# Operand sums of the feed-forward activations: where they are made, how they are loaded, and the PSUM ring of the gate and up products

## The reference, cut to what matters

```python
h = _layer_norm(x) * (1 + sc2) + sh2
a = jax.nn.silu(jnp.einsum('bsd,df->bsf', h, w_gate[l])) * jnp.einsum('bsd,df->bsf', h, w_up[l])
ffn = jnp.einsum('bsf,fd->bsd', a, w_down[l])
x = _layer_norm(ALPHA * x + (1 + g2) * ffn) * ln2_g[l] + ln2_b[l]
```

## Time and profile before

| | |
|---|---|
| Runs shown | 3025.06, 3025.84, 3032.81 us |
| Profiled execution, its own time | 3028.47 us |
| Its span from first to last instruction | 3026.7 us |
| Mean granted TensorE clock | 0.974 |
| Busy: PE, DVE, ACT, POOL | 95%, 74%, 45%, 51% of the span |

### The profile page before, as it was taken

How to read it: one execution, slowest core, us unless ns; L and a number is a source line. 1 busy time by engine, 2 the same in 40 slices (tenths; PEclk the granted TensorE clock), 3 DMA queues, 4 the chain that set the end, 5 groups by cost and what they waited for, 6 DMA issues and landing times.

```text
span 3026.7 us, 39892 instructions
## 1 busy us (share of the span) xinstructions
PE 2862.5 (95%) x13947; PEld 2399.7 (79%) x13947; DVE 2245.8 (74%) x3042; ACT 1365.1 (45%) x2442; POOL 1541.0 (51%) x1179
## 2 busy tenths in 40 slices
PE   7999998999999988999899989999999999999885
PEld 3888886666666656888799989999999978877764
DVE  5666665988888865466776688778766677799877
ACT  3111113777777765365634343434443442323344
POOL 0223321011111125578666677677766675567786
PEclk9999999999999998999999999999999999999997
DMA  7444437121312106376432345556333265567433
GB/s 260 129 132 132 132 111 191 36 70 56 82 56 70 49 22 232 109 234 227 172 111 95 127 139 177 178 175 215 107 104 101 94 222 192 200 222 244 142 125 105
DMA packets 271059, 421.93 MB, mean 139 GB/s; under 512 B 19142, under 2 KB 157063, under 8 KB 264842
## 3 DMA queue, kind: packets, MB, share of 16 engines
q1 hardware_dynamic: 270860, 419.37, 42.6%
HBM read 289.52 MB, written 129.78 MB: 139 GB/s over the span
## 4 chain that ended last, share of the span: by engine, by line
PE 39%; DVE 9%; DVEq 4%; POOL 4%; POOLq 2%; issue 2%; DMA 1%; ACT 1%; SPq 1%; ACTq 0%
PE tail_bank L2482 9%; PE tail_bank L2483 9%; PE tail_bank L2484 9%; PE tail_bank L2508 2%; PE tail_bank L2509 2%; PE tail_bank L2510 2%; PE tail_bank L2415 1%; PE tail_bank L2414 1%; PE tail_bank L2413 1%; POOL tail_rounded L2247 1%; DVE tail_plain L2739 1%; POOL tail_rounded L2226 1%; DVEq L2731 1%; DVE tail_plain L2742 1%; DVEq L2712 1%
## 5 line engine op out<-in xcount | busy, mean ns | idle before, releaser
L2226 POOL TENSOR_TENSOR tail_rounded<-tail_plain,tail_rounded 128x512 fp32r<-128x512 f32 x462 | 660.1, 1442 | 298.6 <-ACT tail_rounded L1989 298.4
L2482 PE MATMUL tail_bank<-tail_rounded 128*128 128x384 f32 x1848 | 625.6, 339 | 32.5 <-DVE tail_plain L2659 26.1
L2483 PE MATMUL tail_bank<-tail_rounded 128*128 128x384 f32 x1848 | 623.3, 337 | 0.0
L2484 PE MATMUL tail_bank<-tail_rounded 128*128 128x384 f32 x1848 | 623.0, 337 | 0.0
L1989 ACT ACTIVATE tail_rounded<-tail_plain 128x512 fp32r<-128x512 f32 x462 | 285.9, 631 | 469.0 <-PE tail_bank L2484 270.9
L2659 DVE TENSOR_TENSOR tail_plain<-tail_plain,tail_bank 128x384 f32<-128x384 f32 x462 | 248.2, 549 | 190.6 <-PE tail_bank L2484 180.3
L2482 PEld LDWEIGHTS tail_bank<-tail_rounded 128*128 128x128 f32 x1848 | 351.3, 190 | 38.5 <-issue 37.8
L2483 PEld LDWEIGHTS tail_bank<-tail_rounded 128*128 128x128 f32 x1848 | 351.7, 190 | 0.0
L2484 PEld LDWEIGHTS tail_bank<-tail_rounded 128*128 128x128 f32 x1848 | 351.5, 190 | 0.0
L1154 DVE TENSOR_REDUCE att_peak<-att_sc 128x1 f32<-128x1024 f32 x256 | 312.8, 1222 | 42.0 <-PE att_sc L966 35.5
L2508 PE MATMUL tail_bank<-tail_rounded 128*128 128x512 f32 x693 | 282.7, 408 | 47.3 <-POOL tail_rounded L2247 30.1
(11 more groups left out here) (289 smaller groups left out, 5547.4 us busy)
## 6 DMA issues: line engine op xcount, KB each, us to landing
tail_plain<-in_w_gu SPq DMA_DIRECT2D x134, 512.0 KB, 4.9
scr_a_d<-tail_plain SPq DMA_DIRECT2D x132, 192.0 KB, 2.1
tail_plain<-scr_a_d SPq DMA_DIRECT2D x18, 1024.0 KB, 5.3
scr_out_d<-tail_plain SPq DMA_DIRECT2D x18, 1024.0 KB, 4.8
tail_plain<-scr_out_d SPq DMA_DIRECT2D x18, 1024.0 KB, 6.9
proj_ada<-in_w_ada SPq DMA_DIRECT2D x16, 1024.0 KB, 6.8
held_w_hi<-scr_qs_d SPq DMA_DIRECT2D x128, 128.0 KB, 2.9
scr_h_d<-tail_plain SPq DMA_DIRECT2D x63, 256.0 KB, 4.4
```

The costliest lines, as they stand in the source:

```text
L2226: nc.gpsimd.tensor_tensor(w_lo[:, j, :], operand(F, j), w_hi[:, j, :].bitcast(F32), ALU.subtract).then_inc(wlo_done, 1)
L2482: nc.tensor.matmul(dst, w_hi[:, j, cols], h_hi(b, j)[:, k, :], start=(k == 0), stop=False)
L2483: nc.tensor.matmul(dst, w_hi[:, j, cols], h_lo(b, j)[:, k, :], start=False, stop=False)
L2484: m = nc.tensor.matmul(dst, w_lo[:, j, cols], h_hi(b, j)[:, k, :], start=False, stop=(k == 3))
```

## The change

It does five things.

- **Sums.** `sums_a(G)` is new and runs once a step on DVE, behind `multiply(G, 3)`. Its four operations of 128x384 make s3, a21 + a22, s2 and s4 from the four blocks in `sils[G % 2]`; s3, s2 and s4 are written over three of the four blocks of `up`. `sums2` and its 27 calls are gone.
- **Stores.** `store_a` stores seven blocks a step instead of four. The first `take_u` of the next up phase waits until the three sums of the step before are stored (`s_stored`), since it writes over them. `a_d` gets the layout operand, row, pair.
- **Loads.** `load_a(r)` loads one operand of one unit (256 KB or 192 KB) into a ring of 12 places; each place is free when POOL has made the low half of the operand 12 back. 189 loads instead of 27. ACT waits for its operand's load instead of for a sum.
- **PSUM ring.** The products of gate and up go through six banks at first (24 products) and then all eight, in one sequence with those of the down stage. `place_read` gives PE the event that frees a bank, and `part_taken` counts the takes in place of the four `bank_read`.
- **rstd.** `rstd(u)` does both tiles of a unit in one set of three operations on two columns. It waits for the variance of both. `normalise(u, c)` waits for that.

```diff
-        a_in = [cut_plain(at, P, "t n", t=4, n=4) for at in (0, 4096)]
-        s2, s3, s4 = (ahead[:, i, :].rearrange("p (t z) -> p t z", z=P) for i in range(3))
+        a_in = [plain[:, at + i * 512:at + (i + 1) * 512] for at in (0, 4096) for i in range(4)] + [ahead[:, i, :] for i in range(4)]
+        SLOTS = len(a_in)
+        SUM_PLACE = ((1, 1), (0, 1), (1, 0))
...
+        def ring_place(n):
+
+            return 2 + n % 6 if n < 24 else (n - 22) % 8
...
             def store_a(G):
...
+                sp.wait_ge(asum_done, 4 * G + 1)
+                store(2, sums[0]).then_inc(s_stored, 16)
+                sp.wait_ge(asum_done, 4 * G + 2)
+                store(5, sil[:, 0, 1, :]).then_inc(a_stored[G % 2], 16)
+                sp.wait_ge(asum_done, 4 * G + 3)
+                store(1, sums[1]).then_inc(s_stored, 16)
+                sp.wait_ge(asum_done, 4 * G + 4)
+                store(6, sums[2]).then_inc(s_stored, 16)
...
-            def load_a(u):
-
+            def load_a(r):
+
+                u, p = divmod(r, OPERANDS)
                 c, q = divmod(u, QUEUE)
...
-                    sp.wait_ge(a2lo_done, OPERANDS * (u - 1))
...
+                elif r >= SLOTS:
+                    sp.wait_ge(a2lo_done, r - SLOTS + 1)
...
             for u in range(UNITS):
-                if u + 2 < UNITS:
-                    load_a(u + 2)
+                for r in range(SLOTS + OPERANDS * u, min(SLOTS + OPERANDS * (u + 1), OPERANDS * UNITS)):
+                    load_a(r)
...
-            def rstd(u, c):
-                n = tile_number(u, c)
-                at = mv[:, n % 4, :]
-                pool.wait_ge(var_done, n + 1)
-                nc.gpsimd.tensor_scalar(at[:, 2:3], at[:, 1:2], 1.0 / D, EPS, ALU.mult, ALU.add)
+            def rstd(u):
+                n = tile_number(u, 1)
+                at = mv[:, n % 4:n % 4 + 2, :]
+                pool.wait_ge(var_done, n + 2)
+                nc.gpsimd.tensor_scalar(at[:, :, 2], at[:, :, 1], 1.0 / D, EPS, ALU.mult, ALU.add)
...
-                    bank = j % 4
-                    if j == 4:
-                        pe.wait_ge(x_done, F + 1)
-                    elif j > 4:
-                        pe.wait_ge(bank_read[bank], 2 * F + 1)
-                    elif F:
-                        pe.wait_ge(bank_read[bank], F if bank in (0, 3) else 2 * F)
-                    dst = gu[:, bank, 0:HALF]
+                    if OPERANDS * F + j > 1:
+                        pe.wait_ge(*place_read(OPERANDS * F + j))
+                    dst = part_bank(F, j)
...
+            def sums_a(G):
+
+                a11, a21, a12, a22 = (sils[G % 2][:, i, c, :] for i, c in ((0, 0), (0, 1), (1, 0), (1, 1)))
+                s3, s2, s4 = (up[:, i, c, :] for i, c in SUM_PLACE)
                 dve.drain()
+                nc.vector.tensor_tensor(s3, a11, a21, ALU.subtract).then_inc(asum_done, 1)
                 dve.drain()
+                nc.vector.tensor_tensor(a21, a21, a22, ALU.add).then_inc(asum_done, 1)
                 dve.drain()
+                nc.vector.tensor_tensor(s2, a21, a11, ALU.subtract).then_inc(asum_done, 1)
+                dve.drain()
+                nc.vector.tensor_tensor(s4, a12, s2, ALU.subtract).then_inc(asum_done, 1)
...
                 if 0 < G < END:
                     sums_w(F + 2)
-                if G == END:
-                    sums2(0)
+                if G:
+                    dve.wait_ge(s_stored, 48 * G)
                 take_u(F + 1, up)
...
                 multiply(G, 3)
+                sums_a(G)
                 beside(4)
...
-                if u + 1 < UNITS:
-                    sums2(u + 1)
```

More of the change, by code:

```diff
@@ L1408, in fourier_to_end @@
         prod_done, x_done, silu_done = s.sem("prod_done"), s.sem("x_done"), s.sem("silu_done")
-        bank_read = [s.sem(f"bank{i}_read") for i in range(4)]
+        part_taken = s.sem("part_taken")
         mult_done = s.sem("mult_done")
@@ L1522, in a2_raw, with place_read, part_bank @@
         def a2_raw(p, u):
-            n, tile = pairs_in(u), a_in[u % 2]
-            return (tile[:, 0:n, 0], s2[:, 0:n], s3[:, 0:n], tile[:, 0:n, 1], tile[:, 0:n, 3], tile[:, 0:n, 2], s4[:, 0:n])[p]
+            return a_in[(OPERANDS * u + p) % SLOTS].rearrange("p (t z) -> p t z", z=P)[:, 0:pairs_in(u)]
         def a2_ready(p, u):
-            if p in (0, 3, 4):
-                return a2_landed[u % 2], 16 * (u // 2 + 1)
-            return s_done, 4 * u + {2: 1, 5: 2, 1: 3, 6: 4}[p]
+            r = OPERANDS * u + p
+            return a2_landed[r % SLOTS], 16 * (r // SLOTS + 1)
         def a2_free(p, u):
             return (down_done, OPERANDS * (u - 1) + p + 1) if u else (prod_done, OPERANDS * (PHASES - 1) + A_FREE[p])
+        def ring_place(n):
+            return 2 + n % 6 if n < 24 else (n - 22) % 8
+        def place_read(n):
+            before = [m for m in range(max(0, n - 8), n) if ring_place(m) == ring_place(n)]
+            if not before:
+                return {2: (tp_done, NT - 4), 3: (tp_done, NT - 4), 4: (gated1, NT - 1), 5: (gated1, NT - 1)}.get(
+                    ring_place(n), (h2_done, NT) if ring_place(n) < 2 else (gated1, NT))
+            if before[-1] < FIRST_DOWN:
+                F, j = divmod(before[-1], OPERANDS)
+                return (part_taken, (OPERANDS - 1) * F + j) if j else (x_done, F + 1)
+            u, p = divmod(before[-1] - FIRST_DOWN, OPERANDS)
+            return (taken, (OPERANDS - 1) * u + p) if p else (first_done, u + 1)
+        def part_bank(F, j):
+            return bank[:, ring_place(OPERANDS * F + j), 0:HALF]
         def out_bank(n):
-            return bank[:, (6, 7, 0, 1, 2, 3, 4, 5)[n % 8], :]
+            return bank[:, ring_place(FIRST_DOWN + n), :]
         def out_place(u):
@@ L1862, in step @@
                         load_piece(m)
-                    load_a(0)
-                    load_a(1)
+                    for r in range(SLOTS):
+                        load_a(r)
                     for m in range(STAGE, 4 * OPERANDS):
@@ L2024, in silu @@
             def silu(G, i, c):
-                bank, reads = {(0, 0): (3, 2 * G + 1), (1, 0): (0, 2 * G + 1), (1, 1): (1, 4 * G + 2), (0, 1): (2, 4 * G + 2)}[i, c]
-                act.wait_ge(bank_read[bank], reads)
+                act.wait_ge(part_taken, (OPERANDS - 1) * 2 * G + 3 + A_ORDER.index((i, c)))
                 tile = sils[G % 2][:, i, c, :]
@@ L2328, in _ @@
             scale(UNITS - 2, 0)
-            for c in (1, 0):
-                rstd(UNITS - 1, c)
+            rstd(UNITS - 1)
         @block.tensor
```

90 lines of the change are left out of this document (37 added, 53 removed).

## The result

The changed kernel takes 2996.28 us (median of 4 runs, 2994.77 to 3006.12) against 3025.45 us for the kernel before on the same chip: a ratio of 0.9905, interval 0.9879 to 0.9931. The change gains 29 us where 68.5 were forecast, and the time lies outside the range.

A forecast was written before the change was run, and what follows sets the result against it. PE was taken to set the time, losing to waits on POOL and DVE and a lower clock. Savings of 40 + 12 + 5 + 5.5 + 6 = 68.5 us gave 2960.0, forecast as 2957 us for the runs' median; range 2938 to 2988.

The forecast's parts named there:

- Third pass, -40 us: Rest of pass 2, down stage: operands arrive as loads and rstd merges, so POOL's 19.0 us unit fits PE's 19.1; 40 us saved.
- Rival (1): POOL and ACT bound pass 2, with a POOL unit of 22.6 us; 18 to 28 us come back, 2980 us; 13%.
- Second change of pass, -12 us: Change to pass 2: without `sums2` DVE enters in step with PE; 3.4 of 15.4 us lost remain, 12 us saved.
- Transfers: Added stores and operand loads on SP's queue cost nothing; DMA engines in pass 1 go from 0.62 to about 0.73 busy.
- Rival (4): An operand waits for a load behind stores; pass 2 keeps a third of its loss, changes keep theirs: 2990 us; 5%.
- Tail, -5.5 us: Behind PE's last matmul: early POOL leaves one take and one join, less the cost of held rstd; 5.5 us saved.
- Gate and up, -6 us: Gate and up: the longer ring's gain and the added sums' cost together save 6 us, between -14 and +10.
- No PE time in the steady steps: Steady steps of gate and up: the sums, 3.6 us a step, fit DVE's slack of 9.5 and 6.8 us.
- +1 to +3 us saved at each: Changes of block in gate and up: the ring gives and the sums take, netting 1 to 3 us saved at each.
- rival (2): Every sum in gate and up meets POOL, 6.3 us a step; steps and changes pay 24 us: 2981 us; 13%.
- rival (3): The ring removes all 26.1 us of bank waits and their low clock, saving 20 to 25 us: 2941 us; 14%.
- rival (5): Sums ahead of weight sums lengthen all 33 steps of gate and up, 119 us against 62.5 gained: 3082 us; 3%.

The follow-up runs named there:

- turn_later: The changed kernel with the eleven steps of `turn_down` moved from all of block 1 to steps 13 to 19 and 24 to 27: 2986.5 us.
- sums_next: The changed kernel with the four sums of a step placed behind the third take of the next step: 3020.0 us.

## Why the prediction was wrong

The forecast is 39 us too low; against the profiled execution it is 2995.9 - 2960.0 = 35.9 us. Of these 3.1 are the later start of gate and up. The terms (they add up to some 38; the counts of windows that touch each other take the matmuls at their common edge twice, 2092 in the windows of the earlier trace rows for the down stage against 2079 in the program, so losses by window come out a little low):

- **Third pass, -40 us: right.** Its loss of 40.8 us is gone (149.3 - 657 x 0.2275 = 0), though PE's margin came from the lead and not from POOL's pace. POOL's unit was forecast at 19.0 us and is 20.2: the rstd is cheaper than allowed (1.7 us with its gaps instead of 2.6), but the scales took 3.39 us each and not 2.60, and the low halves 1.6 and not 1.46, with DVE beside them. Rival (1) had the right engine; the lead of up to 19.1 us pays for some eight units of 1.1 us, by the trace with some 3 us to spare at the end.
- **Second change of pass, -12 us: 2 came.** It lost 15.4 us and loses 13.6 (45.0 - 138 x 0.2275). DVE did enter the change early, as forecast: it reached the first piece at 2771.36, with the stage 6.5 us later than before, where it had been at 2775.90. Then it stood idle for 6.66 us ahead of the low half at 2786.28, because ACT had no piece to round. The failed step is **Transfers**: "both at nothing" asked only whether operands and next weights come in time, and not what the new loads are issued ahead of. Here the weight pieces of the next pass stood behind them. The DMA engines were also fuller than forecast in pass 1, busy 0.82 of 2668 to 2770 and not 0.73. Rival (4) had the queue, and that the changes would keep their loss, but the wrong transfer, and in pass 2 no loss came of it.
- **First change of pass, -5 us: nothing came.** 6.2 us were lost and 6.6 are (46.0 - 173 x 0.2275), with 7.5 us of ACT's waiting for pieces: the same cause. The reordering gave 9.5 us at both. With it the two would have reached 11 of the 17 us.
- **First unit: right.** 11.4 us were lost, 12.2 are.
- **Tail, -5.5 us: it lost 4.6.** "With POOL early, shift is early, and behind PE's end stand one take and one join" failed: POOL, at 20.2 us a unit, is late at the end. The shift ahead of the last takes came 2.9 us later against PE's end than before, and it waited 1.70 us for POOL's scale. Behind PE's end DVE then had a shift, the takes and both joins. The common rstd, which waits for both tiles, costs 1.6 to 1.8. With the shifts out of the way the tail is 3.1 us shorter; no run removed POOL's lag, so its share of the rest stays open.
- **Gate and up, -6 us: it lost 3.6.** The prediction gave only what the ring and the sums come to together. At the start and at the first change this was right: 2.6 and 1.3 us saved. Two steps failed. **"No PE time in the steady steps"**: the steps 13 to 20 lose 3.4 us more than before. By ACT's copies each of the steps 12 to 19 takes 29.5 us or more instead of 29.1, by the prediction's own sign ("longer than 29.1 us") a miss. The steps of blocks 0 and 2, which have the sums but not `turn_down`, lose nothing, and neither do those of block 1 without the sums. So each of the two fits into a step by itself, as was read from the earlier trace rows, and both together do not. In turn_later, where `turn_down` begins at step 13, the steps 13 to 16 lose nothing and the steps 18 and 19 some 0.8 us each: what reserve there is gets used up over several steps. **"+1 to +3 us saved at each" change**: the second one loses 4.0 us more, because the sums cost 10.4 us there and the ring and the rest gave 6.5. The same prediction had a row of 42.56 us busy of 47 for a change of block, and named no price for the sums in it. The granted clock in the window of the second change is 0.94.
- **Rivals (2) and (3).** The sums cost 23.0 us in all: rival (2), at 24, agreed in its sum by luck, since a sum of four additions cost DVE 3.0 us a step, not 6.3, and the loss lay elsewhere (3.4 us in the steps of block 1 and not 11, 10.4 at the second change and not 6.3, 4.0 at the start). The ring gave 11.5 to 15.2 us, with 4.4 more not separated: rival (3), at 20 to 25, was near the 19.6 us of the two. I had treated these two as alternatives to the forecast and to each other, and both came true at once.
- **Slower, rival (5).** The change stayed clear of it, but by one place in DVE's order (sums_next).

## What to carry to other kernels

Price an added operation at the place where its engine is fullest, not in the steady state, and price what hides delays (a longer ring) and what adds them (new work on the late engine) separately, since both can come in full. A reserve that was read with one extra load in place is not free for a second one. A load that is early enough itself can still be late for others: list what is issued behind it on its queue at the busiest moment. If one engine falls a little behind per unit and a buffer hides it, the lag is paid at the end; look for it in the tail.

## What was not expected of the hardware

- Undisturbed operations on POOL of a few elements cost the same for two columns as for one in these traces: the set took 0.19 + 0.70 + 0.53 us on 128x2, and 0.19 + 0.54 + 0.68 us on 128x1. The second set of the same unit took 1.22 + 0.54 + 1.09 us on 128x1.
- DVE and POOL slow each other without either showing idle time: the same scale took 2.42 and 3.39 us, the same sum 0.56 and 1.48. Moving 1.7 us of work from POOL to DVE shortened POOL's period by only 0.25 us.
- The landing of 256 KB pieces went from a median of 4.2 us to 6.6, with one of 10.0 us in the chain of waits at the second change of pass, while the down stage as a whole moved 234 GB/s. With the pieces ahead of the operand loads the median is 5.7 us, although the window of that change moved 303 GB/s instead of 249: that speaks for what was issued just before, and not for the rate alone.
